# First attention of a two-block kernel: query units taken in pairs, and transposes turned through three PSUM banks

## What is computed

```python
for l in range(2):
    h = rms_norm(x, norm_g[l])
    c_q, c_kv, k_pe, z_a, u_f, z_f, g_a, g_f = split(h @ w_in[l])
    q, k, v = heads(c_q, c_kv, k_pe)             # 8 heads; q, k: 96 wide, v: 64 wide; norm and rope
    o_a = softmax(q @ k.T * 96 ** -0.5) @ v      # for each head, 1024 x 1024 scores
    y_a = (o_a * silu(z_a)) @ w_attn_proj[l]
    y_f = (fourier(u_f) * silu(z_f)) @ w_fourier_proj[l]
    m = sigmoid(g_a + b[l, 0]) * y_a + sigmoid(g_f + b[l, 1]) * y_f
    x = x + m @ w_out[l]
```

## Time and profile before

| what | value |
|---|---|
| median of 3 runs | 2594.45 us (2590.34 to 2595.15) |
| the profiled execution's own time | 2594.3 us |
| its span on the core | 2592.5 us |
| PE busy | 2470.2 us (95%) |
| DVE, ACT, POOL busy | 1419.3 (55%), 836.0 (32%), 390.0 us (15%) |
| attention with its edges, layer 1 and layer 2 | stretches 212 to 468 and 1095 to 1345 us of the span |
| granted PE clock over the span | 0.987 of full speed |

### The profile page before, as it was taken

One profiled execution on the slowest core, in us unless ns is written; L12 is line 12 of the kernel. 1 busy time (PEld: TensorE's weight loads), 2 busy tenths in 40 slices (PEclk: granted clock), 3 DMA queues, 4 the chain that ended last, 5 costly groups with the idle time before them and its releaser, 6 DMA issues.

```text
span 2592.5 us, 30752 instructions
## 1 busy us (share of the span) xinstructions
PE 2470.2 (95%) x12425; PEld 1809.0 (70%) x12425; DVE 1419.3 (55%) x2274; ACT 836.0 (32%) x1478; POOL 390.0 (15%) x491
## 2 busy tenths in 40 slices
PE   7999998999999999999989999999999989889997
PEld 6857887788777787688868887776556545644553
DVE  2356777342223343477753322234789999777762
ACT  3344545231113142454451311131442103333341
POOL 0014320100000001233110000000325672300000
PEclk9999999999999999999999999999999999999998
DMA  5010000311113211000011111124000011200000
GB/s 204 29 49 1 2 1 4 89 45 44 45 39 130 65 70 44 33 1 2 1 53 38 49 49 49 57 98 137 35 10 33 4 39 41 98 17 33 17 23 26
DMA packets 106382, 116.83 MB, mean 45 GB/s; under 512 B 20705, under 2 KB 78785, under 8 KB 106241
## 3 DMA queue, kind: packets, MB, share of 16 engines
q1 hardware_dynamic: 105088, 110.66, 13.7%
q10 hardware_dynamic: 1152, 4.19, 0.4%
HBM read 96.82 MB, written 16.84 MB: 44 GB/s over the span
## 4 chain that ended last, share of the span: by engine, by line
PE 84%; DVE 9%; ACT 3%; POOL 2%; issue 1%; SPq 1%; DMA 1%; DVEq 0%; POOLq 0%; ACTq 0%
PE PS L656 7%; PE PS L659 7%; PE PS L662 7%; PE PS L597 6%; PE PS L488 5%; PE PS L621 4%; PE PS L1038 4%; PE PS L607 4%; PE PS L799 4%; PE PS L709 2%; PE PS L722 2%; PE PS L533 2%; PE PS L728 2%; PE PS L725 2%; PE PS L1009 2%; DVE R2a L2135 2%
## 5 line engine op out<-in xcount | busy, mean ns | idle before, releaser
L656 PE MATMUL PS<-hHi,R2bR 128*128 128x512 f32 x768 | 301.5, 393 | 7.3 <-POOL hHi L2328 7.3
L659 PE MATMUL PS<-hLo,R2bR 128*128 128x512 f32 x768 | 300.8, 392 | 0.0
L662 PE MATMUL PS<-hHi,R2bR 128*128 128x512 f32 x768 | 300.6, 391 | 0.0
L1826 DVE TENSOR_TENSOR R2bR<-W,R2bR 128x1024 fp32r<-128x1024 f32 x48 | 61.9, 1312 | 267.8 <-ACT R2bR L1354 267.7
L656 PEld LDWEIGHTS PS<-hHi,R2bR 128*128 128x128 f32 x768 | 145.3, 189 | 39.7 <-POOL hHi L2328 9.0
L1419 ACT ACTIVATE R3a<-PS,pT 128x512 f32<-128x512 f32 x64 | 42.3, 687 | 403.6 <-PE PS L662 403.5
L1805 DVE TENSOR_REDUCE negm<-PS 128x1 f32<-128x1024 f32 x128 | 156.5, 1223 | 27.7 <-PE PS L597 22.1
L1370 ACT ACTIVATE R2b<-PS,negm 128x1024 f32<-128x1024 f32 x128 | 142.3, 1112 | 78.4 <-DVE negm L1805 78.4
L799 PE MATMUL PS<-hT,W 128*128 128x512 f32 x384 | 167.1, 596 | 0.0
L662 PEld LDWEIGHTS PS<-hHi,R2bR 128*128 128x128 f32 x768 | 145.3, 189 | 30.3
L659 PEld LDWEIGHTS PS<-hLo,R2bR 128*128 128x128 f32 x768 | 145.2, 189 | 30.1
(11 more groups left out here) (389 smaller groups left out, 4906.6 us busy)
## 6 DMA issues: line engine op xcount, KB each, us to landing
W<-in_w_in SPq DMA_DIRECT2D x10, 2048.0 KB, 8.5
W<-in_w_in SPq DMA_DIRECT2D x33, 512.0 KB, 4.7
xres<-R SPq DMA_DIRECT2D x3, 4096.0 KB, 18.0
W<-in_w_out SPq DMA_DIRECT2D x6, 2048.0 KB, 7.8
R<-xres SPq DMA_DIRECT2D x2, 4096.0 KB, 18.0
R<-in_x ACTq DMA_DIRECT2D x8, 512.0 KB, 7.8
W<-in_w_in SPq DMA_DIRECT2D x4, 1024.0 KB, 6.9
R3a<-rsums SPq DMA_DIRECT2D x16, 256.0 KB, 5.4
```

The source lines that it names most:

```text
L656: mm = pe.matmul(o, wHi[c % 2][:, k, :], hHi[:, k, ns], start=(k == 0), stop=False)
L659: mm = pe.matmul(o, wHi[c % 2][:, k, :], hLo[:, k, ns], start=False, stop=False)
L662: mm = pe.matmul(o, wLo[c % 2][:, k, :], hHi[:, k, ns], start=False, stop=(k == 7))
```

## The change

Three things change in the attention of both layers, and one in the merge stage.

1. PE works by pairs: scores of units 2p+2 and 2p+3, V products of the pair before, then the transposes of unit 2p, the q/k turns due at this pair, and the transposes of unit 2p+1. `Pb` gets four buffers instead of two, the additional two in weight slot 0, and for the last head in the space of `q_tok`. Slot 0's next load waits until unit 58 for that.
2. Every turn, of P or of q/k, is one fill of a ring of three banks (4, 5, 7); `turn_plan` gives each fill its bank and count. Of each unit's P, ACT copies the first half and DVE the second. DVE's `head_out` and `rest_of_h`, and ACT's `round_h` and `in_place`, stand ahead of the pair's maxima and exponentials. ACT rounds five rows of h in the loop instead of four.
3. POOL's waits for the stage buffer are on the q/k copies.
4. In the merge stage, all rounded products of the four groups come first and the plain ones after them, with the wait on `s_yback` between.

The diff, cut to its core (`bk.turn` looks a fill up in the plan; the helpers of the head-0 turns, POOL's waits and the bookkeeping of counts are left out):

```diff
+def qk_steps(h):
+    return [1, 1, 2, 2] if h == 1 else [4 * h - 6 + i for i in range(4)]
...
+def turn_plan():
+    ring, plan, n = (4, 5, 7), {}, 0
+    for p in range(UNITS // 2):
+        fills = [("p", 2 * p, j) for j in range(2)] + [("qk", *x) for x in QK_TURNS[p]]
+        for f in fills + [("p", 2 * p + 1, j) for j in range(2)]:
+            plan[f] = (ring[n % 3], n // 3)
+            n += 1
...
@@ PE
+                def turn(o, fill, src):
+                    b, n = bk.turn(*fill)
+                    pe.wait_ge(free[b], n)
+                    for j in range(4):
+                        mm = pe.transpose(PS[:, b, j * P:(j + 1) * P], src(j), ident[:, :])
+                    mm.then_inc(full[b], 1)
...
-                for u in range(UNITS + 1):
-                    if u + 1 < UNITS:
-                        scores(u + 1)
-                    if u >= 2 and u % 2 == 0:
-                        pv_pair(u - 1)
-                    if u in QK_TURNS:
-                        qk_turn(*QK_TURNS[u])
-                    if u < UNITS:
-                        p_turn(u)
+                scores(1)
+                for p in range(UNITS // 2 + 1):
+                    u = 2 * p
+                    if u + 2 < UNITS:
+                        scores(u + 2)
+                        scores(u + 3)
+                    if p >= 1:
+                        pv_pair(u - 2)
+                    if u < UNITS:
+                        p_turn(u)
+                        for x in QK_TURNS[p]:
+                            qk_turn(*x)
+                        p_turn(u + 1)
...
@@ ACT
+                exponential(0)
+                exponential(1)
+                for p in range(UNITS // 2):
+                    u, j = 2 * p, p - (UNITS // 2 - 5)
+                    if j >= 0:
+                        round_h(j)
+                    if j >= 1:
+                        in_place(j - 1)
+                    if u + 2 < UNITS:
+                        exponential(u + 2)
+                        exponential(u + 3)
+                    p_copy(u)
+                    for x in QK_TURNS[p]:
+                        qk_copy(*x)
...
+                    p_copy(u + 1)
...
@@ DVE
+                maximum(0)
+                maximum(1)
+                for p in range(UNITS // 2):
+                    u, j = 2 * p, p - (UNITS // 2 - 5)
+                    if p >= 5 and p % 4 == 1:
+                        head_out(p // 4 - 1)
+                    if j >= 1:
+                        rest_of_h(j - 1)
+                    if u + 2 < UNITS:
+                        maximum(u + 2)
+                        maximum(u + 3)
+                    p_copy(u)
+                    for x in QK_TURNS[p][:-1]:
+                        qk_rest(*x)
+                    p_copy(u + 1)
+                    for x in QK_TURNS[p][-1:]:
+                        qk_rest(*x)
...
@@ PE, merge stage
+                    for br, n, b in groups:
+                        x = [oT, fT][br - 2]
+                        rest_ = [j for j in range(4 * (br - 2), 4 * (br - 1)) if m > Y_LAST[j]]
+                        for j in rest_:
+                            mm = pe.matmul(PS[:, b, :], g[:, 16 + j, :], x[:, j % 4, n * 512:(n + 1) * 512],
+                                           start=(j == rest_[0] and b not in last), stop=(j == rest_[-1]))
```

More of the change, by code:

```diff
@@ L121, in skip, with turn, attention @@
             self.n[i % 8] += 1
+    def turn(self, *fill):
+        b, i = TURNS[fill]
+        return b, self.n[b] + i
+    def attention(self):
+        for b in (4, 5, 7):
+            self.n[b] += N_TURNS
 class Steps:
@@ L689, in _ @@
                     pe.wait_ge(s_ywlo, l * KD + m + 1)
+                    groups = [(br, n, 4 * n + br) for br in range(2, 4) for n in range(2)]
+                    last, first = {}, True
+                    for br, n, b in groups:
+                        o = begin(b)
+                        whole = all(m <= Y_LAST[j] for j in range(4 * (br - 2), 4 * (br - 1)))
+                        for j in range(4 * (br - 2), 4 * (br - 1)):
+                            if m <= Y_LAST[j]:
+                                wh, hi, lo = y_weights_hi(l, m, j, j + 1), yHi[j], yLo[j]
+                                ns = slice(n * 512, (n + 1) * 512)
+                                mm = pe.matmul(o, wh, hi[:, ns], start=(b not in last), stop=False)
+                                if first:
+                                    mm.then_inc(s_wdone, 1)
+                                first = False
+                                pe.matmul(o, wh, lo[:, ns], start=False, stop=False)
+                                last[b] = j
+                                mm = pe.matmul(o, y_weights(WR, l, m, j, j + 1), hi[:, ns], start=False,
+                                               stop=(j % 4 == 3 and whole))
+                        if whole:
+                            mm.then_inc(full[b], 1)
@@ L1337, in qk_copy @@
                 def qk_copy(h, i):
-                    o = arrive(turn_bank(h, i))
+                    if h == 0:
+                        o = arrive(4 + i)
+                    else:
+                        b, n = bk.turn("qk", h, i)
+                        act.wait_ge(full[b], n + 1)
+                        o = PS[:, b, :]
                     dst = qkT[h % 2][i // 2]
@@ L1354, in round_weights, with exponential @@
                     act.activation(wHi[c % 2], w, ACT.Copy).then_inc(s_whi, 1)
+                def exponential(u):
+                    b = 2 * (u % 2)
+                    bk.take(b)
+                    act.wait_ge(s_nm, l * UNITS + u + 1)
+                    if u == UNITS - NT + 2:
+                        act.wait_ge(s_stage, (l + 1) * 2 * H - 1)
+                    act.activation(Pb(u), PS[:, b:b + 2, :].rearrange("p a c -> p (a c)"), ACT.Exp,
+                                   bias=negm[:, u:u + 1], accum_out=rsum[:, u:u + 1]).then_inc(free[b], 1)
@@ L1382, in _ @@
+                bk.attention()
                 for h in range(H):
                     bk.take(6)
-                for k in range(4, KD):
+                for k in range(5, KD):
                     round_h(k)
@@ new lines, in maximum, with p_copy @@
+                def maximum(u):
+                    b = 2 * (u % 2)
+                    arrive(b)
+                    if u % NT == NT - 1:
+                        sums_ready.append(bk.count(b))
+                    dve.tensor_reduce(negm[:, u:u + 1], PS[:, b:b + 2, :].rearrange("p a c -> p (a c)"), AX.X,
+                                      ALU.max, negate=True).then_inc(s_nm, 1)
+                def p_copy(u):
+                    b, n = bk.turn("p", u, 1)
+                    dve.wait_ge(full[b], n + 1)
+                    dve.tensor_copy(PT[u % 2][:, 512:1024], PS[:, b, :]).then_inc(free[b], 1)
@@ L2322, in _ @@
                                        ).then_inc(s_stage, 1)
-                    for i in range(4):
-                        bk.take(turn_bank(h, i))
+                for b in range(4, 8):
+                    bk.take(b)
+                bk.attention()
                 for k in range(H_ACT, KD):
```

170 lines of the change are left out of this document (59 added, 111 removed).

## The result

The changed kernel takes 2601.93 us, the median of 12 runs (2596.92 to 2604.84), against 2592.76 us for the kernel before on the same chip (12 runs, 2589.85 to 2595.15): a ratio of 1.0031, with a 95% interval of 1.0023 to 1.0038. It is slower by 9.2 us. Predicted were 2604 us and 9.7 us more than the profiled execution's own time.

The account below looks back on a forecast made before the run. PE was taken to set the pace. Per layer 1.9 + 6.5 + 2.8 - 6.0 = +5.2 us, two layers +10.4, less 0.4 for the merge stage, on 2594.3 gives about 2604 us; 8-in-10 range 2592 to 2611.

Parts of the forecast that it names:

- An ordinary pair: Attention pairs with five fills: fill 4 waits for ACT's copy of fill 1, 0.11 us a pair, 1.9 a layer.
- The hand-off of 0.15: Time from a copy's end to the waiting turn, 0.15 us; a surcharge for waiting on two engines was suspected.
- fill 5 in time: In an ordinary pair, fill 5 waits on DVE's copy of fill 2 (5.92 to 6.60) and was called in time.
- The hand-out: DVE's head_out ahead of both maxima delays fill 4 by 1.08 us, for six heads: 6.5 us a layer.
- The first pairs: Start of each layer's attention: waits of 1.4, 2.0, 0.8 and 0.9, 5.1 against 2.3, so +2.8 us.
- The last head: Pairs 26 to 31: big exponential and P-copy waits go, 3.5 us against 9.5, so -6.0 a layer.
- The merge stage: Twelve alternations of plain and rounded products a layer become five: 0, at most -0.5 us over the kernel.
- A change of kind costs nothing to 0.02: Merge stage: switching from plain to rounded matmuls costs PE between 0 and 0.02 us.
- The clock: Rival on attention clock speed: layer 1 loses only what layer 2 does, 5 us come back, 2599 us; chance 0.12.
- The rival that the ring hides the copies: No fill waits for a copy in ordinary pairs or at hand-outs; 2580.5 us, chance 0.10.
- The rival of the cheaper hand-outs: Hand-out copies find DVE ahead by half a microsecond, 3 us a layer stay away: 2598 us, chance 0.10.
- The rival of slower hand-offs: 0.03 us more at each hand-off makes ordinary pairs and starts cost 3 us more a layer: 2610, chance 0.10.

Follow-up runs that it names:

- experiment 6: Changed kernel without PE's wait for the exponential ahead of a P turn, except for the last two units: 2602.45 us, ratio 1.0034.
- experiment 1: Changed kernel with the two P copies of a unit exchanged, DVE copying the first half and ACT the second: 2590.71 us, ratio 0.9995.
- experiment 2: Changed kernel with the hand-out's reciprocal and first copy moved ahead of the previous pair's P copies, only the second copy before the maxima: 2592.29 us, ratio 0.9996.
- experiment 9: Changed kernel with both edits at once, P copy halves swapped between DVE and ACT and the hand-out split: 2592.33 us, ratio 0.9998.
- Experiment 4: Changed kernel with ACT's first P copy of pair 0 ahead of the exponential of unit 3: 2598.90 us, ratio 1.0024.
- experiment 3: Kernel before, with DVE's rest of h and ACT's in_place one unit later in the last head: 2582.35 us, ratio 0.9963.
- experiment 5: Changed kernel with the merge loop of the kernel before, rounded and plain products alternating again: 2602.14 us, ratio 1.0031.
- experiment 10: Kernel 7 with the change's merge-stage order, rounded products first: 2571.5 us, ratio 0.9907.
- kernel 7: Kernel before with the last head's row work one unit later, and the last step of h rows 6 and 7 on ACT instead of POOL: 2570.88 us, ratio 0.9910.
- experiment 8: Changed kernel with the hand-out behind the pair's two maxima instead of ahead of them: 2637.44 us, ratio 1.0169.

## Why the prediction was right

By its own steps:

- **An ordinary pair: right, 0.02 too dear.** Laid out were fill 1 at 4.79, ACT's copy at 5.48, fill 4 at 6.26 and a pair of 7.14; the timeline has 4.83, 5.52, 6.27 and 7.12. The hand-off of 0.15, taken from one row as the least known number, measured 0.15 and 0.14; experiment 6 shows that about half of it is the second wait, as the prediction suspected. It called fill 5 in time; experiment 6 shows that fill 5's chain, over DVE's copy of fill 2, ends so close behind fill 4's that the pair gains nothing when fill 4 alone comes earlier. Seventeen pairs cost 17 x 0.09 = 1.5 us a layer, not 1.9.
- **The hand-out: right.** A hand-out interval and the one ahead of it take 7.18 + 7.94 or 7.35 + 7.95 us, against 2 x 7.03; less one ordinary loss of 0.09 this is 0.97 or 1.15, mean 1.06, against 1.08, so 6.4 us a layer against 6.5. Not foreseen was that V waits there for `head_out`'s second copy, 0.1 to 0.2 us. That wait costs nothing of its own, since the later wait for ACT's copy ends last. Experiments 1 and 2 took these microseconds away by two edits that cut the same chain, and experiment 9 showed that they are one term.
- **The first pairs: right.** 1.4 and 2.0, then 0.8 and 0.9 were given; the waits in the table are 3.4 together, then 8.19 - 7.46 = 0.73 and 8.79 - 7.90 = 0.89. Experiment 4 took 1.4 us off by the order on ACT alone.
- **The last head: right**, -6.0, and its waits of 1.55, 0.9 and 0.9 measured 1.50, 0.98 and 1.09. But the cause is the place of the row work, and not the new order of PE: experiment 3.
- **The merge stage: the size right, its reason not given.** The sum took 0.4 off for both layers, though the paragraph on it ends at 0, at most -0.5, and does not say where 0.4 comes from; the runs have 0.45 (experiments 5 and 10). "A change of kind costs nothing to 0.02" holds for the change itself. What the new order gains goes with the spacing of the rounded matmuls behind it, which the prediction did not look at.
- **The clock.** In the stretch of layer 1 it rose from 0.97 to 1.00 (3.4 us at half speed lie just behind the stretch's end, from 468.4), in layer 2 it stayed at 0.99. The rival expected 5 us back from that. What came back is 1.9: the first 144 matmuls behind layer 1's attention fell from 40.03 to 38.74, and 0.6 at the start. The rest of the half-speed time in the kernel before lay where PE was waiting anyway: its interval of 11.0 us in the last head is as long in layer 2, where the clock was full. Layer 1's first scores came 2.3 us later than before (216.80 against 214.47), which is scatter between executions: in the eleven kernels of the experiments, none of which touches what is ahead of it, they lie between 214.6 and 216.9.

The terms that the traces show make 2 x 4.6 less 0.45 = 8.8 us, where the sum had 10.0; most of the difference is the ordinary pairs. The medians of 12 runs differ by 9.2 us, with an interval of 6.0 to 9.9. That 2604 lies only 2 us above the measured 2601.93 is partly chance: the sum is 1.2 too high and stands on one execution of 2594.3, 1.5 above the median of the 12 runs (2592.76), and what is not accounted for goes the other way.

The rival that the ring hides the copies fell: with a copier that was idle the way from one fill of a bank to the next took 1.53 us, and three banks give 1.31 (experiment 1); with one wait less it was 1.38 (experiment 6). The Trainium skill ("Perfetto Trace Analysis", Matmuls) advises to rotate independent groups through PSUM banks; this case adds that the rotation must be longer than the way through the copy. The rival of the cheaper hand-outs fell with the intervals of 7.94 and 7.95 us. The rival of slower hand-offs fell with the 0.15 and 0.14.

What stays open: whether a ring of four banks would bring the ordinary pair back to 7.03. It wasn't tried, since all eight banks have a use. Nor is it settled what makes the granted clock fall: it did so behind waits of 2.7 to 2.9 us in some pairs and not in others, and in kernels 3 and 7 behind two waits of 0.9 and 0.8 us close together at the end of layer 1's attention (at 443.8 and 443.9), but not behind the same two in layer 2.

## What to carry to other kernels

Where PE hands banks to a copying engine in rotation, compare the full way (the writes of a fill, hand-off, copy, hand-off with every wait that stands there) with the number of banks times the time of a fill: a ring that is shorter makes PE wait at each round, however idle the copier is on average, and any work placed ahead of the producer of that chain (here the hand-out before the maxima) reaches PE once the chain's slack is used up (here 1.06 us of some 1.5). Before a loop's order is redone to get rid of waits at its end, ask which of the other engines' steps make them: here two steps of the row work, moved one unit later, gave all that the new order gained at the end of the attention, and the one wait that neither order touched, on POOL, was worth as much again (11.5 to 12.4 us).

## What the runs showed that was not expected

- Rounded matmuls behind plain ones start up to 0.24 us apart for about ten, and 0.227 apart in a long stream. Neither the change of kind nor the reverse shows a gap.
- A second wait in front of a turn costs 0.07 to 0.09 us at that turn. An ordinary pair was no shorter without it, because the next turn then waited for another copy.
- A stretch that ends at a change from plain to rounded matmuls hides 0.40 us of what the change costs behind its end: the two kernels were 0.66 us a layer apart at the first product with `w_out` and 0.22 from the twentieth on.
- Waits of 2.7 to 2.9 us of PE in the middle of a full stream were followed by 3.4 us at 0.51 of full speed in three and four pairs of a layer (experiment 8), at a cost of up to 1.6 us each beside the wait itself. Waits of 0.8 us at hand-outs were not, but two of 0.9 and 0.8 us within 2 us of each other were, in layer 1 of kernels 3 and 7.
- POOL takes 6.56 us for two element-wise steps of 128 x 1024, ACT 2.94 for three.
